# Retention samples as outer products on VectorE, products in parts, the last projection in thirds

## The chip, the cores and the metric

One core of one Trainium2 chip. The metric is the device time of one execution in microseconds (us), as a median over runs.

## The reference

One inference step of a one-layer decoder for a prompt (1024 tokens) and eight samples of one new token each, with the same weights. Retention and forgetting attention run side by side, are merged, normed, and followed by a convolutional feed-forward network and a second norm. The parts that the change touches, cut down:

```python
def retention_chunkwise(q, k, v, s0):      # 4 heads, dk = 128, dv = 256; chunks of 128 tokens, a sample is a chunk of one
    def step(s, qkv):
        qc, kc, vc = qkv
        inner = einsum('bihd,bjhd->bhij', qc, kc) * intra
        o = einsum('bhij,bjhe->bihe', inner, vc) + einsum('bihd,bhde->bihe', qc * q_decay, s)
        s = s * chunk_decay + einsum('bjhd,bjhe->bhde', kc * k_decay, vc)
        return s, o
def merge_branches(...):                   # group norm of ret_o, silu(rg) * rn; sigmoid(ga) * u_a + sigmoid(gb) * u_b
def conv_ffn(h, ...):                      # a = gelu(conv(h @ w_up)) * (h @ w_gate); a @ w_down, d_ff = 2816
def post_norm_ffn(...):                    # layer_norm(ALPHA * h + f): the norm that ends the step
```

The samples' new states (8 x 4 x 128 x 256) are outputs too. The samples' attention reads 32 pages of 128 cached keys and values each, from a page table.

## The kernel before, in words

Activations are held transposed, `x[128, 8, 1032]` (1024 prompt columns and 8 samples), once as a rounded high part and once as the rest. A product (`product`, L106 to L123) is one tile of 128 output columns of a weight matrix: three chunks of 344 columns, each 8 k-tiles x 3 matmuls (high-high, high-low, low-high), 72 matmuls. Products are numbered as jobs. Their weights go through a ring of two: GpSimd loads a tile (`load_weight`, L89) once the tile two jobs back has been split, ScalarE rounds it (`split_hi`, L97), VectorE takes the rest (`split_lo`, L104), and TensorE starts. Chunk n of a product goes to bank n, and the next product waits until that bank has been read.

`retain` loops over four heads. In a head, jobs 0 and 1 are rq and rk (rotated by VectorE), 2 and 3 a gate, 4 and 5 a second gate, 6 and 7 rv, 8 and 9 rg; jobs 10 to 13 are the next head's 0 to 3, so a pass through the loop holds ten products. After job 7 TensorE turns nine blocks of key and value rows (L941, L943), does eight chunks (scores and state update L968 and L969, output L957 and L959), the eight samples, product 8, nine transposes of the normed rows (L1002), and products 9 to 13. The prompt's state is updated by VectorE (L1232), rows are copied by ScalarE (L1060 to L1068), the group norm is VectorE's (L1255 to L1267) and the copy to `rv_t` ScalarE's (L1084). The samples: VectorE makes a masked copy of the eight key rows (L1242) and of the queries (L1244), TensorE multiplies each masked key block with the value rows (L984), VectorE adds that to the decayed state (L1248), and TensorE sums the outputs over eight masked queries (L989).

Between these, in fixed doses (`VALUES_A`, `KEYS_A`, `VALUES_B`, `KEYS_B`: so many groups at each place of the program), VectorE scores cached keys (L1118, L1122) and TensorE multiplies cached values (L889), groups of two pages that SyncE loads into rings of four.

`finish` ends with the feed-forward network in three sections of 8, 7 and 7 of the 22 tiles; each ends with a down projection of eight products that VectorE adds to `acc` (L1720). After the last, nine row blocks are turned by TensorE (L1490, two buffers), measured by VectorE (L1739), normed by ScalarE (L1589), scaled by VectorE (L1731), and get their bias from GpSimd (L1439).

## Time and profile before

| | |
|---|---|
| median of 3 runs | 2246.5 us (2238.74 to 2246.7) |
| the profiled execution, own time | 2241.36 us |
| its span, first to last instruction | 2239.7 us |
| TensorE busy | 2054.5 us (92%) |
| VectorE, ScalarE, GpSimd busy | 1148.9, 614.5, 211.2 us |
| mean granted clock of TensorE | 0.949 of full speed |
| moved by DMA | 266.09 MB, 119 GB/s over the span |

A matmul's busy time overlaps the next one's; what one costs is read from the distance of their starts. The granted clock has two values here, 1.0 (2.4 GHz) and 0.5 (1.2 GHz), and a stretch shows their mean. Its records lie some us behind the matmuls that they slow down.

### The profile page before, as it was taken

To read this page: it belongs to the slowest core of one execution; us is meant where nothing else is said; L and a number is where in the kernel's file an instruction comes from. 1 tells how busy PE (TensorE), PEld (TensorE's weight loads), DVE (VectorE), ACT (ScalarE), POOL (GpSimd) and SP (SyncE) were. 2 spreads that over 40 slices of the span, in tenths; PEclk is the share of its full clock that TensorE was granted. 3 is DMA by queue.
4 is the path that set the end of the run, shared out by engine and by line. 5 is a ranking of instruction groups with operands and counts; after the bars stand their busy time and mean duration, and the time that the engine had idled before them with its cause. 6 is when DMAs were issued, how large, how long until landed. Compare 5 with 4: busy or idle time off the path is not lost. (4 is left out here: it accounts for less than half of the span.)

```text
span 2239.7 us, 39810 instructions
## 1 busy us (share of the span) xinstructions
PE 2054.5 (92%) x14403; PEld 1887.1 (84%) x14403; DVE 1148.9 (51%) x1754; ACT 614.5 (27%) x1127; POOL 211.2 (9%) x241
## 2 busy tenths in 40 slices
PE   7998998798998999899869899699999999999995
PEld 6887888686886787698669889599999999999995
DVE  4645546866847756676432575833332333233326
ACT  4444432123122222222220100444411232023213
POOL 1000000110110020011000010300000000000003
PEclk9999999898999999899879999899999999999997
DMA  4111113693876678489442321011111111111111
GB/s 133 48 38 39 39 38 124 220 320 128 305 264 215 212 257 290 141 285 318 155 158 86 111 86 43 0 57 47 47 47 47 47 47 42 53 42 43 58 46 76
DMA packets 127296, 266.09 MB, mean 119 GB/s; under 512 B 18329, under 2 KB 31734, under 8 KB 127150
## 3 DMA queue, kind: packets, MB, share of 16 engines
q1 hardware_dynamic: 97130, 168.87, 22.1%
q0 software_dynamic: 21856, 78.18, 11.6%
q10 hardware_dynamic: 8192, 17.40, 2.1%
q8 instruction: 82, 1.34, 0.3%
q14 instruction: 36, 0.29, 0.0%
HBM read 236.27 MB, written 28.22 MB: 118 GB/s over the span
## 5 line engine op out<-in xcount | busy, mean ns | idle before, releaser
L121 PE MATMUL bank<-x_hi,w_hi 128*128 128x344 f32 (+1 forms) x2328 | 770.3, 331 | 61.4 <-DVE w_lo L104 16.0
L121 PE MATMUL bank<-x_lo,w_hi 128*128 128x344 f32 (+1 forms) x2328 | 754.5, 324 | 0.0
L121 PE MATMUL bank<-x_hi,w_lo 128*128 128x344 f32 (+1 forms) x2328 | 754.4, 324 | 0.0
L121 PEld LDWEIGHTS bank<-x_hi,w_hi 128*128 128x128 f32 (+1 forms) x2328 | 445.3, 191 | 90.1 <-issue 80.8
L121 PEld LDWEIGHTS bank<-x_lo,w_hi 128*128 128x128 f32 (+1 forms) x2328 | 445.0, 191 | 1.6
L121 PEld LDWEIGHTS bank<-x_hi,w_lo 128*128 128x128 f32 (+1 forms) x2328 | 444.8, 191 | 1.7
L121 PE MATMUL bank<-moving_hi,w_hi 128*128 128x344 f32 x912 | 283.0, 328 | 26.5 <-DVE moving_lo L1595 14.3
L97 ACT ACTIVATE w_hi<-w_raw 128x1024 fp32r<-128x1024 f32 (+2 forms) x145 | 148.6, 1025 | 534.5 <-PE bank L121 491.2
L121 PE MATMUL bank<-moving_lo,w_hi 128*128 128x344 f32 x912 | 292.8, 321 | 0.0
L121 PE MATMUL bank<-moving_hi,w_lo 128*128 128x344 f32 x816 | 263.3, 323 | 0.0
L104 DVE TENSOR_TENSOR w_lo<-w_raw,w_hi 128x1024 fp32r<-128x1024 f32 (+2 forms) x145 | 171.9, 1186 | 138.4 <-ACT w_hi L97 132.8
L121 PEld LDWEIGHTS bank<-moving_hi,w_hi 128*128 128x128 f32 x912 | 170.1, 191 | 36.5 <-issue 16.3
L121 PEld LDWEIGHTS bank<-moving_lo,w_hi 128*128 128x128 f32 x912 | 172.7, 189 | 0.1
L1118 DVE TENSOR_TENSOR cache_keys<-cache_keys,q_wide 128x1024 f32<-128x1024 f32 x128 | 156.5, 1223 | 23.3 <-DMA cache_keys<-in_cache_k_dram 23.3
L121 PEld LDWEIGHTS bank<-moving_hi,w_lo 128*128 128x128 f32 x816 | 155.5, 191 | 0.0
L1122 DVE TENSOR_REDUCE score<-cache_keys 128x16 f32<-128x1024 f32 x128 | 154.8, 1212 | 0.0
L1698 DVE SCALAR_TENSOR_TENSOR stage<-stage,conv_cols_tile 128x1024 f32<-128x1024 f32 x22 | 28.3, 1285 | 186.0 <-ACT stage L1560 186.0
L1720 DVE TENSOR_TENSOR acc<-acc,bank 128x344 f32 (+1 forms) x72 | 36.9, 513 | 168.3 <-PE bank L121 168.3
L89 POOL DMA_DIRECT2D w_raw<-in_w_in_dram x53 | 49.7, 938 | 774.1 <-DVE w_lo L104 585.2
L889 PE MATMUL bank<-cache_vals,score 128*2 128x128 f32 x2048 | 81.5, 278 | 3.0 <-DMA cache_vals<-in_cache_v_dram 2.9
L1708 DVE TENSOR_TENSOR stage<-stage,bank 128x344 f32<-128x344 f32 x66 | 33.8, 512 | 94.8 <-PE bank L121 92.6
L1555 ACT ACTIVATE stage<-bank 128x344 f32<-128x344 f32 x66 | 30.0, 456 | 155.0 <-PE bank L121 155.0
(247 smaller groups left out, 2206.6 us busy)
## 6 DMA issues: line engine op xcount, KB each, us to landing
cache_keys<-in_cache_k_dram SPq DMA_DIRECT2D x256, 256.0 KB, 5.0
cache_vals<-in_cache_v_dram SPq DMA_DIRECT2D x256, 256.0 KB, 5.2
w_raw<-in_w_in_dram POOLq DMA_DIRECT2D x52, 512.0 KB, 7.1
w_raw<-in_w_up_dram POOLq DMA_DIRECT2D x22, 512.0 KB, 4.5
w_raw<-in_w_gate_dram POOLq DMA_DIRECT2D x22, 512.0 KB
gate_t_scratch<-rv_rows ACTq DMA_DIRECT2D x16, 516.0 KB, 4.8
gate<-gate_t_scratch SPq DMA_DIRECT2D x16, 516.0 KB, 3.5
w_raw<-in_w_down_dram POOLq DMA_DIRECT2D x16, 448.0 KB, 4.2
```

Source lines behind the costliest of these rows:

```text
L89: eng.dma_start(g.w_raw[slot][:, 0:kt, 0:m], src).then_inc(g.w_land[slot], 16)
L97: act.activation(g.w_hi[slot][:, 0:kt, 0:m], g.w_raw[slot][:, 0:kt, 0:m], ACT.Copy).then_inc(g.w_rounded, 1)
L104: dve.tensor_tensor(g.w_lo[slot][:, 0:kt, 0:m], g.w_raw[slot][:, 0:kt, 0:m], g.w_hi[slot][:, 0:kt, 0:m].bitcast(F32), ALU.subtract).then_i ...
L121: mm = pe.matmul(g.bank[n][0:m, 0:TC], w[slot][:, k, 0:m], x[:, k, chunk(n)], start=(k == 0 and i == 0), stop=(k == kt - 1 and i == 2))
L889: mm = pe.matmul(bank[7][32 * j:32 * j + 2, 0:P], score[u][:, i * GRP + p, 2 * j:2 * j + 2], vals[slot][:, p, j * P:(j + 1) * P], start=(f ...
L1118: dve.tensor_tensor(keys[slot][:], keys[slot][:], qb[u][:].unsqueeze(1).to_broadcast([P, GRP, FH * HD]), ALU.mult).then_inc(k_mult, 1)
L1122: dve.tensor_reduce(score[u][:, (i - 1) * GRP:i * GRP, :], keys[slot][:].rearrange("p g (h e) -> p g h e", e=HD), AX.X, ALU.add).then_inc( ...
L1555: act.activation(up[:, 2 + k * TC:2 + (k + 1) * TC], bank[k][:, 0:TC], ACT.Copy).then_inc(g.bank_free[k], 1)
L1698: dve.scalar_tensor_tensor(act_in[:, 0:SEQ], up[:, 1:1 + SEQ], fc[:, 17:18], act_in[:, 0:SEQ], ALU.mult, ALU.add).then_inc(conv, 1)
L1708: dve.tensor_tensor(act_in[:, chunk(k)], act_in[:, chunk(k)], bank[k][:, 0:TC], ALU.mult).then_inc(g.bank_free[k], 1)
L1720: dve.tensor_tensor(cols, cols, bank[k][:, 0:TC], ALU.add).then_inc(g.bank_free[k], 1)
```

## The change

1. **Samples.** The samples' value rows go to HBM and come back as two transfers that put four of the rows into every partition (into `inner` and `qd`, which the chunks no longer need then). ScalarE scales the old states, VectorE adds key column x value row (one instruction a sample). The outputs come from matmuls with two columns each in four column groups of the array; the query tile `q_pair` has zeros in the other column.
2. **Parts.** Products 6 to 9 are cut into 24 parts of three matmuls, which stand between the row transposes, the chunks, the samples and the norm's transposes. The second gate's jobs change places with rv's, and the gates are activated and stored chunk by chunk.
3. **Thirds, bias.** The last section's down projection runs over 384, 384 and 264 columns one after the other, each with all eight output tiles (24 jobs with a load and a split each); the rows of a finished third are turned, normed, scaled and get their bias (GpSimd) during the next.

The doses of cached keys and values are moved to fit. The diff, cut (the lines left out rename sizes and drop the masks' constants):

```diff
+def product_part(g, pe, jb, xh, xl, i, kt=KD, m=P):
+    j, slot = jb
+    n, k = i // kt, i % kt
+    if i == 0:
+        pe.wait_ge(g.w_split, RING + j + 1)
+    if k == 0:
+        pe.wait_ge(g.bank_free[n], j + 1)
+    for q, (w, x) in enumerate(((g.w_hi, xh), (g.w_hi, xl), (g.w_lo, xh))):
+        mm = pe.matmul(g.bank[n][0:m, 0:TC], w[slot][:, k, 0:m], x[:, k, chunk(n)],
+                       start=(k == 0 and q == 0), stop=(k == kt - 1 and q == 2))
+    if k == kt - 1:
+        mm.then_inc(g.mm_chunk, 1)
...
-VALUES_A = (1,) * 12 + (1,) * 3 + (1,) + (0,) * 6
-KEYS_A = (1,) * 12 + (1,) * 3 + (1,) + (0,) * 6
-VALUES_B = (0, 1) + (1,) * 3 + (0,) * 3 + (1,) * 12
-VALUES_B_LAST = (2,) * 8 + (0,) * 12
+PARTS = NCH * KD
+VALUES_A = (1, 2, 1, 1, 2, 1) + (0, 1, 1, 0, 1, 1, 0, 1, 1) + (1, 0, 1, 0, 0, 0, 0)
+KEYS_A = (1, 2, 1, 1, 2, 1) + (0, 1, 1, 0, 1, 1, 0, 1, 1) + (1, 0, 1, 0, 0, 0, 0)
+VALUES_B = (1, 1, 1, 1) + (0, 0, 0) + (1,) + (1,) * 7 + (2, 2)
+VALUES_B_LAST = (2,) * 8 + (0,) * 9
...
-        kmask = inner[0:NS]
-        qmask = sb("q_own", [P, NS, NS])
+        spread = [x[:].rearrange("p t d -> p (t d)").rearrange("p (b d) -> p b d", d=DV) for x in (inner, qd)]
+        HALF, GROUPS = NS // 2, 4
+        q_pair = sb("q_own", [P, NS, 2])
...
-        COLS = (C_RQ, C_RK, C_GA, C_GA + P, C_GB, C_GB + P, C_RV, C_RV + P, C_RG, C_RG + P)
+        COLS = (C_RQ, C_RK, C_GA, C_GA + P, C_RV, C_RV + P, C_GB, C_GB + P, C_RG, C_RG + P)
...
-                    for j in (8, 9):
-                        load(h, j)
+                    load(h, 8)
+                    wait_apart(pool, rows_out, (h + 1) * NB, g.mm_chunk)
+                    pool.dma_start(g.v_dram[ds(h, 1)].rearrange("a b d -> (a b) d"), vrows[0:NS, QB, :]).then_inc(v_spread, 16)
+                    load(h, 9)
+                    wait_apart(pool, v_spread, h * 48 + 16, g.mm_chunk)
+                    wait_apart(pool, o_mm, h * NB + QB, g.mm_chunk)
+                    for i in range(2):
+                        rows = g.v_dram[ds(h, 1), i * HALF:(i + 1) * HALF].rearrange("a b d -> a (b d)").to_broadcast([P, HALF * DV])
+                        pool.dma_start(spread[i].rearrange("p b d -> p (b d)"), rows).then_inc(v_spread, 16)
...
+                    parts(6, share(PARTS, NB, 0))
...
+                        if t:
+                            parts(6, share(PARTS, NB, t))
...
+                    parts(7, range(3))
...
+                        if t < QB - 1:
+                            parts(7, range(3 * t + 3, 3 * t + 6))
...
-                    pe.wait_ge(masks, h * 2 + 2)
-                    pe.wait_ge(st_new, (h + 1) * QB)
-                    for b_ in range(NS):
-                        if b_ >= 2:
-                            pe.wait_ge(s_new, h * NS + b_ - 1)
-                        pe.matmul(bank[4 + b_ % 2][:, 0:DV], kmask[:, b_, :], vrows[0:NS, QB, :], start=True, stop=True).then_inc(kv_s, 1)
+                    parts(8, range(4))
+                    for i in range(2):
+                        parts(8, range(4 + 4 * i, 8 + 4 * i))
                     values_b(0)
                     pe.wait_ge(o_out, h * NB + QB)
-                    for b_ in range(NS):
-                        pe.wait_ge(s_new, h * NS + b_ + 1)
-                        mm = pe.matmul(bank[3][0:NS, 0:DV], qmask[:, b_, :], st_s[:, b_, :], start=(b_ == 0), stop=(b_ == NS - 1))
+                    pe.wait_ge(masks, h + 1)
+                    for i in range(2):
+                        pe.wait_ge(s_new, h * NS + (i + 1) * HALF)
+                        for j in range(GROUPS):
+                            b_ = i * HALF + j
+                            mm = pe.matmul(bank[3][32 * j:32 * j + 2, 0:DV], q_pair[:, b_, :], st_s[:, b_, :], start=(i == 0), stop=(i == 1))
                     mm.then_inc(o_mm, 1)
                     values_b(1)
-                    product(g, pe, job(h * NJ + J0, 1, 8), g.xh, g.xl, after=lambda n: values_b(2 + n))
+                    parts(8, range(12, PARTS))
+                    values_b(2)
+                    parts(9, range(8))
+                    values_b(3)
 
                     for t in range(NB):
-                        n = P if t < QB else NS
+                        n = P
                         b = bank[3] if t % 2 == 0 else bank[6]
+                        if t < 8:
+                            parts(9, (8 + t,))
...
+                    parts(9, range(16, PARTS))
+                    values_b(7)
...
+                def gate_chunk(j, i, h, tile, n):
+                    b = i % 2
+                    act.wait_ge(gate_stored[b], h * 96 + (16 * (i // 2) + 1))
+                    chunk_ready(g, act, j, n)
+                    act.activation(sg[b][:], bank[n][:, 0:TC], ACT.Sigmoid).then_inc(g.bank_free[n], 1)
+                    act.wait_ge(g.bank_free[n], j + 2)
+                    act.dma_start(g.gate_dram[ds(tile, 1), :, chunk(n)].rearrange("a p t -> (a p) t"), sg[b][:]).then_inc(gate_stored[b], 16)
...
+                        if t < NS:
+                            act.activation(st_s[:, t, :], st_s[:, t, :], ACT.Copy, scale=hc[:, RDEC]).then_inc(s_scaled, 1)
+                        if t in (1, 4, 6):
+                            gate_chunk(h * NJ + (J0 + 7), 9 + (1, 4, 6).index(t), h, h * 2 + (KD + 1), (1, 4, 6).index(t))
                         if t == QB - 1:
                             cache_exp(h * 2 + 1, 1)
                             nxt(8)
+                            for b_ in range(2):
+                                act.wait_ge(gate_stored[b_], h * 96 + 97)
+                            silu(0)
...
+                    silu(1)
+                    nxt(9)
...
+                    silu(2)
+                    silu(3)
+                    store_gated(0)
+                    silu(4)
+                    silu(5)
+                    store_gated(1)
...
-                    dve.wait_ge(o_mm, h * NB + QB)
-                    dve.tensor_tensor(kmask, krows[0:NS, QB, :].unsqueeze(1).to_broadcast([NS, NS, DK]),
-                                      own[:].unsqueeze(2).to_broadcast([NS, NS, DK]), ALU.mult).then_inc(masks, 1)
-                    dve.tensor_tensor(qmask[:], rqT[:, SEQ:T].unsqueeze(1).to_broadcast([P, NS, NS]), own_col[:], ALU.mult).then_inc(masks, 1)
-                    dve.wait_ge(s_land, h * 16 + 16)
+                    for i in range(2):
+                        pair = slice(i * HALF, (i + 1) * HALF)
+                        ins = dve.tensor_copy(q_pair[:, pair, i], rqT[:, SEQ + i * HALF:SEQ + (i + 1) * HALF])
+                    ins.then_inc(masks, 1)
+                    dve.wait_ge(v_spread, h * 48 + 48)
                     for b_ in range(NS):
-                        dve.wait_ge(kv_s, h * NS + b_ + 1)
-                        dve.scalar_tensor_tensor(st_s[:, b_, :], st_s[:, b_, :], hc[:, RDEC], bank[4 + b_ % 2][:, 0:DV], ALU.mult, ALU.add).then_inc(s_new, 1)
+                        dve.wait_ge(s_scaled, h * NS + b_ + 1)
+                        dve.scalar_tensor_tensor(st_s[:, b_, :], spread[b_ // HALF][:, b_ % HALF, :], rkT[:, SEQ + b_:SEQ + b_ + 1],
+                                                 st_s[:, b_, :], ALU.mult, ALU.add).then_inc(s_new, 1)
...
+    JT, KT = sections[-1][3], sections[-1][1]
+    THIRD = 3
+    EDGE = (0, 3 * P, 6 * P, T)
+    tail = [(i, i // KD, i % KD) for i in range(NCH * KD)]
+    turned_after = {KD * (t // THIRD + 1) + 1 + 2 * (t % THIRD): t for t in range(2 * THIRD)}
...
+                for i, _, m in tail:
+                    load_weight(g, pool, job(JT, JT % 2, i), tile_of(a["w_down"], m, sections[-1][0], KT), KT)
+                    if i - 6 in turned_after:
+                        add_row(turned_after[i - 6])
+                for t in range(QB):
+                    if t not in [turned_after[i - 6] for i, _, _ in tail if i - 6 in turned_after]:
+                        add_row(t)
...
+                def turn_rows(t):
                     n = P if t < QB else NS
+                    pe.wait_ge(g.bank_free[0], JT + 1 + KD * (t // THIRD + 1))
...
+                for i, third, m in tail:
+                    j, slot = job(JT, JT % 2, i)
+                    lo, hi = EDGE[third], EDGE[third + 1]
+                    pe.wait_ge(g.w_split, RING + j + 1)
+                    if i < NCH:
+                        pe.wait_ge(g.bank_free[i], JT + 1)
+                    else:
+                        pe.wait_ge(g.bank_free[0], JT + 1 + i - NCH + 1)
+                    for k in range(KT):
+                        if i == 0:
+                            pe.wait_ge(a_lo, sections[-1][0] + k + 1)
+                        for q, (w, x) in enumerate(((g.w_hi, gh), (g.w_hi, gl), (g.w_lo, gh))):
+                            mm = pe.matmul(bank[i % NCH][:, 0:hi - lo], w[slot][:, k, :], x[:, k, lo:hi],
+                                           start=(k == 0 and q == 0), stop=(k == KT - 1 and q == 2))
+                    mm.then_inc(g.mm_chunk, NCH)
+                    if i in turned_after:
+                        turn_rows(turned_after[i])
+                for t in range(2 * THIRD, NT):
+                    turn_rows(t)
...
+                for i, third, m in tail:
+                    if i < len(tail) - 1:
+                        split_lo(g, dve, job(JT, JT % 2, i + 1), KT)
+                    lo, hi = EDGE[third], EDGE[third + 1]
+                    chunk_ready(g, dve, JT + i, NCH - 1)
+                    dve.tensor_tensor(acc[:, m, lo:hi], acc[:, m, lo:hi], bank[i % NCH][:, 0:hi - lo], ALU.add).then_inc(g.bank_free[0], 1)
+                    for after, step in ((1, measure_rows), (2, invert_rows), (3, scale_rows)):
+                        if i - after in turned_after:
+                            step(turned_after[i - after])
+                for t in range(2 * THIRD, NT):
+                    measure_rows(t)
+                    scale_rows(t - 1)
+                    invert_rows(t)
```

What it moves. On TensorE, the samples of a head (`state_samples` are the states, `inner_t` held the masked keys). Before:

```order
L959 MATMUL banks<-state,q_decayed_t 128x256
L906 MATMUL bank<-ident,dec_out 128x128
L979 REGISTER_ALU
L980 REGISTER_ALU
L984 MATMUL banks<-rv_rows,inner_t 128x256 x8
L989 MATMUL banks<-state_samples,q_own 8x256 x8
L886 ISA
L889 MATMUL bank<-cache_vals,score 2x128 x8
L112 REGISTER_ALU
L121 MATMUL bank<-x_hi,w_hi 128x344
```

The outer products (L984) and the outputs (L989) stood right behind the last chunk, and product 8 (L121) behind them. Now, between two pieces of product 8 (L138):

```order
L138 MATMUL bank<-x_hi,w_lo 128x344
L138 MATMUL bank<-x_hi,w_hi 128x344
L138 MATMUL bank<-x_lo,w_hi 128x344
L138 MATMUL bank<-x_hi,w_lo 128x344
L904 REGISTER_ALU
L906 ISA
L909 MATMUL bank<-cache_vals,score 2x128 x8
L1020 MATMUL banks<-state_samples,q_own 2x256 x8
L909 MATMUL bank<-cache_vals,score 2x128 x8
L138 MATMUL bank<-x_hi,w_hi 128x344
```

The outer products are gone and the outputs (L1020) have 2 rows each; twelve parts of product 8 stand in front of the samples' outputs, and the other twelve behind.

On TensorE, the group norm's transposes of a head. Before, they stood together, without matmuls between. Now (`cache_vals` is a group of cached values):

```order
L909 MATMUL bank<-cache_vals,score 2x128 x8
L138 MATMUL bank<-x_hi,w_hi 128x344
L138 MATMUL bank<-x_lo,w_hi 128x344
L138 MATMUL bank<-x_hi,w_lo 128x344
L1037 MATMUL banks<-ident,rv_rows 128x128 x2
L138 MATMUL bank<-x_hi,w_hi 128x344
L138 MATMUL bank<-x_lo,w_hi 128x344
L138 MATMUL bank<-x_hi,w_lo 128x344
L1037 MATMUL banks<-ident,rv_rows 128x128 x2
L138 MATMUL bank<-x_hi,w_hi 128x344
L138 MATMUL bank<-x_lo,w_hi 128x344
```

A part of product 9 stands in front of each of the first eight.

On GpSimd, the body of the head loop behind the weight load of job 9, before (`w_raw` is the ring's tile):

```order
L89 DMA w_raw<-in_w_in_dram 128x8x128
L73 REGISTER_ALU
L89 ISA
L89 DMA w_raw<-in_w_in_dram 128x8x128
L73 ISA
L838 ISA
L838 ISA cache_max_all<-cache_max 128x8
```

The load of job 10 and the maximum over all partitions (`cache_max_all`) followed directly. The same place now:

```order
L89 DMA w_raw<-in_w_in_dram 128x8x128
L73 REGISTER_ALU
L73 ISA
L886 DMA inner_t<-own_values_scratch 128x1024
L886 ISA
L886 DMA q_decayed_t<-own_values_scratch 128x1024
L73 REGISTER_ALU
L89 ISA
L89 DMA w_raw<-in_w_in_dram 128x8x128
L73 ISA
L851 ISA
L851 ISA cache_max_all<-cache_max 128x8
```

The two spreads (`own_values_scratch` to `inner_t` and `q_decayed_t`) stand in front of both; the store of the value rows, not shown, went in front of load 9.

On GpSimd, the end of the program (`y` with a number is a block of rows), where before all adds of the bias stood behind the last weight load:

```order
L89 DMA w_raw<-in_w_down_dram 128x7x128 x16
L1510 TENSOR_TENSOR y_9124<-y_9124,ln_wide_9134 128x1024
L89 DMA w_raw<-in_w_down_dram 128x7x128 x2
L1510 TENSOR_TENSOR y_9125<-y_9125,ln_wide_9134 128x1024
L89 DMA w_raw<-in_w_down_dram 128x7x128 x2
L1510 TENSOR_TENSOR y_9126<-y_9126,ln_wide_9134 128x1024
L89 DMA w_raw<-in_w_down_dram 128x7x128 x4
L1510 TENSOR_TENSOR y_9127<-y_9127,ln_wide_9134 128x1024
L1510 TENSOR_TENSOR y_9128<-y_9128,ln_wide_9134 128x1024
```

Three adds stand between the weight loads now.

## Rows read from the trace of the kernel before

**Rows 1.** Busy time by stretch: one pass of the head loop.

```profile
core 0: us, PE busy (x) PEld busy (x) DVE busy (x) ACT busy (x) POOL busy (x), PEclk, DMA share, GB/s
624.50:681.70 57.20, 57.05 (x480) 51.64 (x480) 33.83 (x30) 9.69 (x16) 7.98 (x13) 0.95 0.75 254
681.70:688.70 7.00, 5.70 (x75) 3.66 (x75) 4.71 (x4) 5.29 (x18) 0.00 (x0) 1.00 1.01 376
688.70:705.20 16.50, 14.04 (x97) 10.78 (x95) 11.53 (x26) 2.78 (x9) 0.40 (x1) 1.00 0.76 259
705.20:720.50 15.30, 13.10 (x50) 5.75 (x49) 11.03 (x23) 3.32 (x5) 1.08 (x1) 0.67 0.13 35
720.50:734.00 13.50, 13.50 (x121) 12.19 (x120) 8.11 (x24) 1.51 (x3) 0.00 (x0) 1.00 0.52 167
734.00:740.00 6.00, 3.39 (x22) 1.81 (x18) 0.00 (x0) 5.50 (x16) 0.00 (x0) 1.00 0.00 0
740.00:811.10 71.10, 68.47 (x569) 62.36 (x569) 56.82 (x71) 13.41 (x22) 6.78 (x9) 0.95 0.83 277
811.10:815.10 4.00, 0.04 (x1) 0.01 (x1) 0.59 (x3) 3.35 (x5) 0.00 (x0) 1.00 0.83 308
```

**Rows 2.** Busy time by stretch: last head from its samples, down projection, norm.

```profile
1077.90:1119.10 41.20, 35.27 (x351) 24.54 (x354) 15.89 (x43) 10.61 (x23) 0.00 (x0) 0.83 0.57 184
...
2124.60:2201.40 76.80, 76.68 (x486) 76.39 (x486) 20.22 (x32) 7.66 (x7) 4.86 (x5) 1.00 0.14 44
2201.40:2239.70 38.30, 14.94 (x72) 11.33 (x72) 31.00 (x47) 16.85 (x36) 18.74 (x8) 0.58 0.28 111
```

**Rows 3.** The chain that ended last: start, us, what.

```profile
1472.70 22.66 PE bank L121 x144
```

**Rows 4.** Timeline of TensorE after the loop's end, matmul by matmul.

```profile
625.28 0.49 PE L121 MATMUL bank<-x_hi,w_lo 128*128 128x344 f32 x1
...
625.57 0.49 PE L121 MATMUL bank<-x_hi,w_hi 128*128 128x344 f32 x1
```

**Rows 5.** Timeline of TensorE, two groups of cached values, a chunk apart.

```profile
603.26 0.62 PE L889 MATMUL bank<-cache_vals,score 128*2 128x128 f32 x16
...
607.77 0.62 PE L889 MATMUL bank<-cache_vals,score 128*2 128x128 f32 x16
```

**Rows 6.** Timeline, seams: a state's update, a table load, product 9, `finish`.

```profile
713.69 0.48 DVE L1248 SCALAR_TENSOR_TENSOR state_samples<-state_samples,head_const,banks 128x256 f32<-128x256 f32 x1 [0.37 <-PE banks L984]
...
740.71 1.28 ACT L1093 ACT_TABLE_LOAD   x1
...
742.61 0.63 PE L121 MATMUL bank<-x_hi,w_hi 128*128 128x344 f32 x1 [2.71 <-ACT rot_cos L1093]
...
1141.63 11.58 SPq L1378 DMA_DIRECT2D gated_raw<-gated_t_scratch  x8
```

**Rows 7.** DMA issues: KB each, median us from issue to landing.

```profile
q_wide<-q_new_scratch SPq DMA_DIRECT2D x8, 256.0 KB, 5.4
```

**Rows 8.** Weight loads of L89 within the last down projection (448 KB).

```profile
DMA to landing us min/median/max: 4.2/4.3/4.4
```

**Rows 9.** Timeline, one weight tile's rounding, split, and the next load's issue.

```profile
2132.04 1.06 ACT L97 ACTIVATE w_hi<-w_raw 128x1024 fp32r<-128x1024 f32 x1 [7.71 <-PE bank L121]
...
2133.14 1.23 DVE L104 TENSOR_TENSOR w_lo<-w_raw,w_hi 128x1024 fp32r<-128x1024 f32 x1 [0.47 <-ACT w_hi L97]
...
2135.09 0.96 POOL L89 DMA_DIRECT2D w_raw<-in_w_down_dram  x1 [7.64 <-DVE w_lo L104]
```

**Rows 10.** Timeline of the final norm: scaling (VectorE), bias (GpSimd).

```profile
2206.93 1.22 DVE L1731 TENSOR_TENSOR y<-y,ln_wide 128x1024 f32<-128x1024 f32 x1 [0.22 <-ACT y L1589]
...
2208.25 2.34 POOL L1439 TENSOR_TENSOR y<-y,ln_wide 128x1024 f32<-128x1024 f32 x1 [42.47 <-DVE y L1731]
...
2209.89 1.78 DVE L1731 TENSOR_TENSOR y<-y,ln_wide 128x1024 f32<-128x1024 f32 x1
...
2213.41 1.77 DVE L1731 TENSOR_TENSOR y<-y,ln_wide 128x1024 f32<-128x1024 f32 x1
```

192 lines of the change are left out of this document (101 added, 91 removed).

## The prediction

> **What bounds the kernel now.** I read the page first: TensorE is busy for nearly all of the span, so time can only come from stretches where it idles, runs at its lower clock or does work that something else could have covered. Then I cut one iteration of the head loop of `retain` into its stages with the busy time by stretch [rows 1], the last head and the end of the kernel likewise [rows 2], and went into the timeline only at the seams.
>
> The reader is to see three things in [rows 1]. The first 57.2 us and the stretch from 740.0 to 811.1 are dense products. Between them lie 52.3 us in which TensorE is short of work in small doses: row transposes, the eight retention chunks, then 15.3 us for eight samples at a mean granted clock of 0.67, and 6.0 us of group norm in which it is busy for 3.4. Last, 4.0 us of nothing at the loop's end, after which the next stretch shows a clock of 0.95: 2 x 0.05 x 57.2, or 6 us, at the lower level of 1.2 GHz.
>
> Prices. At 2.4 GHz 144 matmuls take 22.66 us [rows 3], 0.157 each: a product (72) is 11.3 us, a chunk of it (24) 3.77, a part (3) 0.47. At 1.2 GHz one starts every 0.29 us [rows 4]. A group of cached values behind a chunk costs 4.51 (from 603.26 to 607.77, [rows 5]) less 3.77, or 0.75, of which 0.55 is the group.
>
> **The change, part by part.** All sums are against the profiled execution (span 2239.7, own time 2241.4 us); the median of the runs shown is 2246.5, 5.1 more, and I take the gain off that.
>
> *Rows and chunks, products 6 and 7 in parts .* Before, from the first product to the last output 57.2 + 7.0 + 16.5 = 80.7 us. After, TensorE's work is the same: four products 45.2, 3 lost at the low clock, 16 value groups 12.0, nine row transposes at 0.38, eight chunks at 1.52, 0.8 for the tail of the sums; what goes are the waits on ScalarE and VectorE (5.7 and 14.0 us busy in 7.0 and 16.5), what comes are some 17 seams between products and small matmuls, at 0.1 each (half the 0.19 that a value group pays beyond its own 0.55). Sum 78.5: **-2** a head. It would be no more if the parts were free, because before, too, the products themselves ran at full rate.
>
> *Samples.* Gone are the two masks, the eight outer products on TensorE and the eight 8-column matmuls, at the low clock. Now VectorE needs the value rows in all partitions. GpSimd issues two 512 KB spreads, and only after the last chunk's output, since they land in `inner` and `qd`. From that moment (705.2 before): issue 0.9 + 0.9, landing, eight updates at 0.4 (one took 0.48 with overlap, [rows 6]) = 3.2. The landing is not in the trace; the nearest are 4.3 us for 448 KB of weights on the same queue [rows 8] and 5.4 for a 256 KB row spread in the same way while the cache streams [rows 7]. Lower end 3.5 (as for 448 KB without its issue), upper end 8 (twice the bytes of the spread row, its fixed part once); I take 4.5, as the cache stream is idle there (DMA share 0.13). States ready at 0.1 + 1.8 + 4.5 + 3.2 = 9.6. TensorE's cover: 12 parts of product 8 and one group, 5.65 + 0.75 = 6.4. So it waits 3.2. Then the outputs, 16 passes in four column groups, 1 us with seams; a group, the other 12 parts, a group, 8 parts of product 9, a group: 12.2. It arrives at the first normalised row at 22.8; VectorE needs for `nxt(8)`, the first keys and nine statistics about 12 us after the states (19.1 busy in 705.2 to 734.0 less 7 for masks and states), 21.6: no wait. The nine rows, a part with each, at 0.9: 30.5. Before, to the same point (740.0), 15.3 + 13.5 + 6.0 = 34.8: **-4.3**. Moving `all_max` behind the spreads costs nothing here: it is done by 3.2, before the states could start. Queued behind VectorE's wait for the spreads are `nxt(8)` and the statistics; I have counted them.
>
> *Product 9 under the group norm.* Before 71.1 us from 740.0: five products, twelve groups, 2.7 of waiting for the gate activation (742.61, [rows 6]) and the low clock after it. After: four products and a third, 49.0, twelve groups 9.0, 1.0 for the tail; chunk 2 of product 9 still waits for bank 2, which `silu(2)` frees behind the last row and a table load of 1.28 [rows 6], 2.3 us; 0.5 where product 11 catches up with the rotations. Sum 61.8: **-9.3**. This is the term that leans on VectorE: it was busy for 56.8 of the 71.1 us [rows 1], so in 61.8 it is at 92%.
>
> Together -15.6 for each of the first three heads. The last has no product 10 to 13 but all 16 value groups early: -2; 41.2 -> 37.8; and from 1119.1 [rows 2] to the first load of `finish` at 1141.6 [rows 6], 22.5 -> 13.3 (chunk 2 with its wait 6.1, two groups, turn, store): **-14.6**. `retain`: 3 x 15.6 + 14.6 = -61.4.
>
> *Low clock at new seams.* A new wait of 3.2 us followed by 2-column matmuls, and one of 2.3 after the group norm, are like the places before which the trace drops to 1.2 GHz (2.71 us idle at 742.61, then [rows 1] 0.95). One drop costs 6 us at 0.29 in place of 0.157, 2.7 us. Two places, four heads; I count every second one: **+11**.
>
> *Thirds.* The last down projection becomes 24 jobs: 21 matmuls of 384, 384 and 264 columns, 3.68 and 2.6 us by the column from 0.157. Every job loads, rounds and splits its weights again. A slot's cycle is landing 4.3 [rows 8] + 0.1 + 3.05 from the rounding to the next issue (2132.04 to 2135.09, [rows 9]) - 0.28 for 7/8 of the columns = 7.2 for two jobs, 3.6 a job. So thirds one and two run at TensorE's 3.68, the last at the load's 3.6 where TensorE needs 2.6. Of the first job only the last matmuls are left at 2124.6: 15.2 x 3.68 + 8 x 3.6 = 84.7; three iterations in which VectorE measures one row and scales another (1.5 + 1.8) before it can split hold the next job for 1.2 each, GpSimd's adds (2.34, [rows 10]) hold a load for 1.3. Sum 90 against 76.8 [rows 2]: +13. Behind it only rows 6 to 8 are left: six fewer at 3.52 (2209.89 to 2213.41, [rows 10]), less 1.8 for row 5's scaling in front: 38.3 -> 19.1. Net **-6**.
>
> A rule bears on this. In [rows 10] the first scaling takes 1.22, the next 1.78: it begins at 2209.89, GpSimd's add ends at 2210.59, and 1.08 later VectorE is done. So VectorE was held until GpSimd was through. The Trainium skill (SBUF - State Buffer, "SBUF: two separate sides") says the same: the pair of ports is an exclusive lock, and a VectorE operation with two SBUF inputs blocks while GpSimd reads. By it each of the adds now inside the jobs can hold a weight split for up to 2.34 us: four of them, +9, and the tail would be +3 in place of -6. I keep -6, since GpSimd's adds mostly start while VectorE waits for a product; the other is a rival.
>
> Sum: -61.4 + 11 - 6 = -56: 2246.5 - 56 = **2190**.
>
> **Rivals.** A, *the moved product does not come free*: VectorE, at 92%, and the key loads (a DMA share of 0.83 in [rows 1], 0.96 when squeezed into 61.8) set the pace from 740 on; product 9 then gives 3 us in place of 9.3 in each of three heads, +19: 2209. For it: the two rates are so near. Against: no key wait of size stands in this stretch before. B, *all of it*: no new seam drops the clock and the spreads land at 3.5: 2190 - 11 - 4 = 2175. For it: TensorE idled over 2 us within the chunks at a clock of 1.00. C, *the port lock eats the tail*: 2190 + 9 = 2199. D, *no change to speak of*: what TensorE is spared comes back as waits for the cache stream, 2240 to 2252; against it, the share of 0.76 and 0.13 in the chunks and the samples. E, *slower*: interleaved with small matmuls, the products of 6 to 9 run at 1.2 GHz. Price: 288 matmuls x 0.13 = 37 us a head, 149 in all, so 2190 - 11 + 149 = 2328 if all do; it decides from the point at which 45% of them (67 of 149) are slow. Against: in the chunk stretch, with 2.5 us idle, the clock was 1.00 [rows 1]. The Trainium skill (TensorE: Matmul & The Clock Gate, "What's actually happening") has the low clock as the default that activity lifts; it would speak for E only if interleaved work counted as idle, which no row shows. A second page, TensorEngine Tiling ("Key Properties"), says that changing the tiling mode drains the array; the 0.19 around a value group is what the trace shows of that, and it is in the seams.
>
> **The numbers.** Forecast 0.41, A 0.19, B 0.16, C 0.10, D 0.06, E 0.08. Predicted 2190. The upper end adds to the forecast the other half of the clock drops (+11), spreads at 8 us (+14) and part of A: 2220; the lower end is B with a little over: 2170. What lies outside is D, E and the far end of A. Within 0.5% (11 us, what a measurement of this kernel can tell) only D: 0.06; slower 0.08; faster 0.86.
>
> **What would show it.** Right: in a head, rows and chunks at a clock of 1.00 with TensorE over 95% busy; `state_samples` matmuls in 1 us after 2 to 4 us of idling released by VectorE's updates; v_spread landing 4 to 5 us after issue; the head's period 175 us (190.6 before) and 64 instead of 71 us behind the group norm; in the tail, jobs every 3.7 us, TensorE waiting for `w_lo` in the last third, 19 us behind the last product. Wrong: idle time before product 11 or 12 released by the rotations or by key loads (A); granted clock 0.5 inside products 6 to 9 (E); jobs of 5 us in the tail with `w_lo` behind GpSimd's adds (C); period unchanged with DMA share at 1 (D). The forecast itself fails most easily in the wait for the spreads, whose landing no row shows, and in how often the clock falls.

## The result, and the profile after

The changed kernel takes 2220.32 us (median of 4 runs, 2217.56 to 2223.97) against 2244.85 for the kernel before in the same comparison: ratio 0.9906, 95% interval 0.9884 to 0.9927, so it is faster by 21 us (16 to 26) by the ratio; the two medians differ by 24.5. The prediction said 2190 (2170 to 2220). The direction was right; the gain was less than half of the 56 us that were forecast.

The page of the changed kernel: busy times of TensorE to GpSimd.

```profile
span 2215.5 us, 39880 instructions
...
PE 2009.2 (91%) x14335; PEld 1873.5 (85%) x14335; DVE 1159.2 (52%) x1771; ACT 645.5 (29%) x1175; POOL 240.9 (11%) x269
```

TensorE works 45 us less (2054.5 before), but the span fell by 24.2 only: 21 us more in which it idles. The pass of head 1 again, cut at the places of [rows 1] (the columns are the same; stages: two whole products, rows, chunks, then up to the samples' outputs, up to the norm's first transpose, the transposes, the dense part, the loop's turn):

```profile
624.34:654.84 30.50, 30.50 (x272) 27.80 (x273) 20.32 (x18) 3.68 (x8) 9.15 (x11) 0.91 0.70 237
654.84:682.37 27.53, 22.78 (x207) 19.11 (x204) 15.93 (x14) 9.96 (x24) 1.51 (x2) 0.88 0.83 286
682.37:706.15 23.78, 23.78 (x175) 21.04 (x174) 14.30 (x28) 6.04 (x16) 0.00 (x0) 1.00 0.80 271
706.15:721.93 15.78, 8.80 (x70) 6.45 (x72) 4.92 (x14) 5.64 (x9) 2.40 (x4) 0.79 0.37 112
721.93:735.57 13.64, 13.64 (x116) 12.16 (x109) 11.64 (x32) 3.40 (x5) 1.08 (x1) 0.87 0.61 204
735.57:741.10 5.53, 5.28 (x39) 4.61 (x36) 2.41 (x5) 5.12 (x15) 0.88 (x1) 1.00 0.15 21
741.10:806.50 65.40, 58.81 (x523) 53.41 (x523) 55.38 (x70) 12.03 (x19) 6.58 (x8) 1.00 0.83 279
806.50:810.60 4.10, 0.28 (x4) 0.01 (x1) 0.32 (x2) 3.11 (x4) 0.00 (x0) 1.00 1.05 355
```

The chunks (third row) are full, as the parts were meant to make them. Three rows have holes: 4.75 us in the row transposes, 7.0 in front of the samples' outputs, and 6.6 in the dense part (2.6 in the 71.1 us before). The timeline names them, TensorE's waits in head 1 (in brackets: us idle, and what ended it; two more that `rot_sin` ended, 0.48 at 762.65 and 0.95 at 779.99, are not shown):

```profile
661.88 1.03 PE L909 MATMUL bank<-cache_vals,score 128*2 128x128 f32 x16 [3.75 <-DMA cache_vals<-in_cache_v_dram]
...
717.98 1.03 PE L909 MATMUL bank<-cache_vals,score 128*2 128x128 f32 x16 [5.90 <-ACT score L1057]
719.63 0.61 PE L1020 MATMUL banks<-state_samples,q_own 128*2 128x256 f32 x4 [0.62 <-DVE state_samples L1311]
...
744.02 0.42 PE L138 MATMUL bank<-x_hi,w_hi 128*128 128x344 f32 x1 [2.47 <-ACT rot_cos L1087]
...
774.46 0.42 PE L121 MATMUL bank<-x_hi,w_hi 128*128 128x344 f32 x1 [1.91 <-DVE rot_sin L1246]
```

The wait that I had expected in front of the outputs, for the states, is 0.62 us there, and 0.46 in front of their second half. The big one is one instruction earlier: a group of cached values waits 5.90 for the softmax's exponential (L1057). Followed back, first GpSimd, then VectorE:

```profile
706.96 0.56 POOL L886 DMA_DIRECT2D inner_t<-own_values_scratch  x1 [24.80 <-PE banks L988]
707.56 0.55 POOL L886 DMA_DIRECT2D q_decayed_t<-own_values_scratch  x1
708.31 0.91 POOL L89 DMA_DIRECT2D w_raw<-in_w_in_dram  x1 [0.20 <-issue]
716.53 0.39 POOL L851 PARTITION_ALL_REDUCE cache_max_all<-cache_max  x1 [7.32 <-issue]
...
716.96 0.43 DVE L1203 TENSOR_TENSOR score<-score,cache_max_all 128x264 f32<-128x264 f32 x1 [11.19 <-POOL cache_max_all L851]
717.31 0.33 DVE L1219 COPY fox_sample_t<-bank 64x4 f32 x2
717.67 0.24 DVE L1306 COPY q_own<-rq_t 128x4 f32<-128x4 f32 x2
717.82 1.67 DVE L1311 SCALAR_TENSOR_TENSOR state_samples<-inner_t,rk_t,state_samples 128x256 f32<-128x256 f32 x4
```

The maximum over all partitions has its scores since 699.6 and takes 0.39 us by its record, but starts 7.3 us after the weight load in front of it, with nothing shown that it waits for. VectorE stands 11.19 us at it, and the states, whose value rows had landed at about 713, follow behind. The same line on its own shows what fills the 7.3 us (start times of the first and last record):

```profile
L851 POOLq MODIFY_POOL_CONFIG  x2: 37/37/37, 709.5 to 709.5; - x2
L851 POOL PARTITION_ALL_REDUCE cache_max_all<-cache_max x1: 394/394/394, 716.5 to 716.5; - x1
```

GpSimd is set up for this instruction at 709.5 and begins 7.0 us later. In the kernel before the set-up stands at 672.1, long before the scores are ready, and so it is hidden:

```profile
L838 POOLq MODIFY_POOL_CONFIG  x2: 37/37/37, 672.1 to 672.1; - x2
L838 POOL PARTITION_ALL_REDUCE cache_max_all<-cache_max x1: 397/397/397, 699.4 to 699.4; - x1
```

The Trainium skill (GPSIMD Engine Reference, "2.1 Instruction dispatch") says so: the first call of a freshly loaded GpSimd function pays about 6 us between `MODIFY_POOL_CONFIG` and its start, with no instruction visible in the profile. The trace agrees in kind, with 7.0 us; the length differs, and it is paid more than once. The program runs two GpSimd functions in a head, eight multiplications (L876) and the maximum, and the set-up stands at every change between them: the multiplications of the four heads start 8.9, 11.1, 10.4 and 9.7 us after theirs. The next maximum of the same head, with no other function in between, has no set-up record and starts 0.2 us after its scores:

```profile
L851 POOL PARTITION_ALL_REDUCE cache_max_all<-cache_max x1: 1172/1172/1172, 613.6 to 613.6; - x1
```

A rival for the 7.0 us is work that GpSimd might still have with the three transfers issued just in front. Against it: where its function does not change, an operation starts 0.02 us after a weight load's issue (an add at 2176.80 in experiment 4, behind a load of 2175.80 to 2176.78). How the 7.0 us divide was not tested.

The end of the kernel, from the last down projection's first matmul (2100.0) on, took 115.5 us; before it was 118.4 (2121.3 to 2239.7). The jobs took 97.3 in place of 80.1, what follows them 18.2 in place of 38.3. The rows of it that matter, VectorE's splits beside GpSimd's adds:

```profile
2155.10 3.16 POOL L1510 TENSOR_TENSOR y<-y,ln_wide 128x1024 f32<-128x1024 f32 x1 [4.08 <-DVE y L1843]
...
2154.93 1.08 DVE L104 TENSOR_TENSOR w_lo<-w_raw,w_hi 128x896 fp32r<-128x896 f32 x1
2156.63 2.58 DVE L104 TENSOR_TENSOR w_lo<-w_raw,w_hi 128x896 fp32r<-128x896 f32 x1
...
2166.68 0.59 PE L1583 MATMUL bank<-moving_hi,w_hi 128*128 128x264 f32 x1 [2.90 <-DVE w_lo L104]
```

### The profile page after: what moved, and what is told of

Same layout as the page of the kernel before. It is cut to its first block and busy times, and to the rows that moved or that the text cites. A ratio compares the mean times of both kernels' runs of the same rounds, so it can differ in the third digit from the quotient of the medians.

```text
span 2215.5 us, 39880 instructions
## 1 busy us (share of the span) xinstructions
PE 2009.2 (91%) x14335; PEld 1873.5 (85%) x14335; DVE 1159.2 (52%) x1771; ACT 645.5 (29%) x1175; POOL 240.9 (11%) x269
## 3 DMA queue, kind: packets, MB, share of 16 engines
q0 software_dynamic: 25184, 89.75, 13.5%
## 5 line engine op out<-in xcount | busy, mean ns | idle before, releaser
L121 PE MATMUL bank<-x_hi,w_hi 128*128 128x344 f32 (+1 forms) x1944 | 639.6, 329 | 58.6 <-DVE w_lo L104 18.3
L121 PE MATMUL bank<-x_lo,w_hi 128*128 128x344 f32 (+1 forms) x1944 | 629.3, 324 | 0.0
L121 PE MATMUL bank<-x_hi,w_lo 128*128 128x344 f32 (+1 forms) x1944 | 629.3, 324 | 0.0
L121 PEld LDWEIGHTS bank<-x_hi,w_hi 128*128 128x128 f32 (+1 forms) x1944 | 370.6, 191 | 77.6 <-issue 65.7
L121 PEld LDWEIGHTS bank<-x_lo,w_hi 128*128 128x128 f32 (+1 forms) x1944 | 370.4, 191 | 1.6
L121 PEld LDWEIGHTS bank<-x_hi,w_lo 128*128 128x128 f32 (+1 forms) x1944 | 370.3, 190 | 1.7
L97 ACT ACTIVATE w_hi<-w_raw 128x1024 fp32r<-128x1024 f32 (+3 forms) x161 | 163.0, 1012 | 574.8 <-PE bank L121 386.9
L121 PE MATMUL bank<-moving_hi,w_hi 128*128 128x344 f32 x744 | 229.9, 331 | 25.4 <-DVE moving_lo L1708 13.7
L104 DVE TENSOR_TENSOR w_lo<-w_raw,w_hi 128x1024 fp32r<-128x1024 f32 (+3 forms) x161 | 192.3, 1194 | 110.4 <-ACT w_hi L97 98.4
L121 PE MATMUL bank<-moving_lo,w_hi 128*128 128x344 f32 x744 | 239.4, 322 | 0.0
L121 PE MATMUL bank<-moving_hi,w_lo 128*128 128x344 f32 x648 | 210.0, 324 | 0.0
L121 PEld LDWEIGHTS bank<-moving_hi,w_hi 128*128 128x128 f32 x744 | 139.0, 192 | 35.0 <-issue 16.1
L138 PE MATMUL bank<-x_hi,w_hi 128*128 128x344 f32 x384 | 142.5, 371 | 8.0 <-ACT rot_cos L1087 8.0
L121 PEld LDWEIGHTS bank<-moving_lo,w_hi 128*128 128x128 f32 x744 | 141.4, 190 | 0.1
L138 PE MATMUL bank<-x_lo,w_hi 128*128 128x344 f32 x384 | 127.7, 333 | 0.0
L138 PE MATMUL bank<-x_hi,w_lo 128*128 128x344 f32 x384 | 127.7, 332 | 0.0
L121 PEld LDWEIGHTS bank<-moving_hi,w_lo 128*128 128x128 f32 x648 | 124.3, 192 | 0.0
L89 POOL DMA_DIRECT2D w_raw<-in_w_in_dram x53 | 49.9, 943 | 634.4 <-DVE w_lo L104 431.0
```

What stands on the lines that cost most here:

```text
L89: eng.dma_start(g.w_raw[slot][:, 0:kt, 0:m], src).then_inc(g.w_land[slot], 16)
L97: act.activation(g.w_hi[slot][:, 0:kt, 0:m], g.w_raw[slot][:, 0:kt, 0:m], ACT.Copy).then_inc(g.w_rounded, 1)
L104: dve.tensor_tensor(g.w_lo[slot][:, 0:kt, 0:m], g.w_raw[slot][:, 0:kt, 0:m], g.w_hi[slot][:, 0:kt, 0:m].bitcast(F32), ALU.subtract).then_i ...
L121: mm = pe.matmul(g.bank[n][0:m, 0:TC], w[slot][:, k, 0:m], x[:, k, chunk(n)], start=(k == 0 and i == 0), stop=(k == kt - 1 and i == 2))
L138: mm = pe.matmul(g.bank[n][0:m, 0:TC], w[slot][:, k, 0:m], x[:, k, chunk(n)], start=(k == 0 and q == 0), stop=(k == kt - 1 and q == 2))
```

## The experiments

All ratios are to the kernel before, run beside each on the same chip; one step of 0.001 is 2.2 us, and the intervals are about 0.002 wide to each side, 0.004 in experiments 9, 10 and 11. The changed kernel, experiments 1 to 4, 5 to 8, 9 to 11 and 12 come from a comparison each; the difference of two ratios is uncertain by some 5 or 6 us, and by some 10 with one of 9 to 11.

**1. The maximum in front of the spreads.** One line of GpSimd's program is moved.

```diff
                     load(h, 9)
+                    all_max(h * 2 + 1)
                     wait_apart(pool, v_spread, h * 48 + 16, g.mm_chunk)
...
                         load(h, NJ)
-                    all_max(h * 2 + 1)
```

> Only GpSimd's order is changed: the maximum over all partitions of the second sample's scores is issued in front of the two spreads instead of behind them. Theory 1 (queue order): in the profile of the changed kernel the value group in front of the samples' outputs waits 5.8 to 6.5 us a head for the softmax's exponential, which waits for that maximum, and the maximum is done 9.6 us after the last chunk because the spreads' issue stands in front of it. Moved, it is done at about the last chunk's end; then TensorE waits for the states only, which follow the spreads' landing: 3.7 us in place of 7.5 a head, so 15 us less, 2205 (ratio to the kernel before 0.982). Theory 2 (the spreads are the wait anyway): VectorE would stand at the spreads as long as it stands at the maximum now, 2217 to 2221 and no change.

Measured: 2195.0, ratio 0.9804 (0.9787 to 0.9820), against 0.9906: 23 us of gain from one line, more than the 15 expected. The waits for the exponential are gone, and TensorE waits for the states, 1.96 and 0.46 us in the first head, 1.98 and 0.88 in the second. All waits in front of the samples' outputs come to 2.4 to 2.9 us a head, where the theory had 3.7. Stage by stage, 20.6 of the 22.0 us that `retain` gained lie between the last chunk's output and the last norm transpose (7.4, 4.3, 5.7 and 3.2 in the four heads). VectorE, freed of its 11 us at the maximum, also no longer comes late with the rotations behind the norm (0.48, 1.91 and 0.95 us of waiting for them in head 1 of the changed kernel, none above 0.4 here). But that is worth little: from the last norm transpose to the next pass head 1 takes 68.5 us in place of 69.3, since the granted clock there is 0.94 in place of 1.00:

```profile
729.20:797.24 68.04, 61.19 (x522) 55.93 (x522) 55.82 (x72) 14.54 (x22) 6.58 (x8) 0.94 0.86 289
```

The theory of queue order holds, and the late rotations of head 1 came from VectorE's being held earlier.

**2. Even doses.**

```diff
-VALUES_A = (1, 2, 1, 1, 2, 1) + (0, 1, 1, 0, 1, 1, 0, 1, 1) + (1, 0, 1, 0, 0, 0, 0)
-KEYS_A = (1, 2, 1, 1, 2, 1) + (0, 1, 1, 0, 1, 1, 0, 1, 1) + (1, 0, 1, 0, 0, 0, 0)
+VALUES_A = (1,) * 6 + (0, 1, 1, 0, 1, 1, 0, 1, 1) + (1, 1, 1, 1, 0, 0, 0)
+KEYS_A = (1,) * 6 + (0, 1, 1, 0, 1, 1, 0, 1, 1) + (1, 1, 1, 1, 0, 0, 0)
```

> Only the doses of cached keys and values in the first stretch of a head are changed: one group a chunk in products 4 and 5 (6 in place of 8), and the two left over go into the retention chunks. Theory 1 (SyncE's rate): SyncE issues four pairs of groups in 2.2 us each and then pauses 6 to 7 us at its loop's turn, so it feeds one group each 3.8 us at best; eight groups in the 30 us of two products are right at that, and TensorE waits 4.0 to 7.2 us a head for cached values. Evened, most of it goes, and the clock drops behind these waits too: 12 to 20 us less, 2200 to 2208. Theory 2 (the stream's total): the same waits come back in the row transposes or the chunks, 2217 to 2221.

Measured: ratio 0.9900 (0.9883 to 0.9918), no change. My theory fell: the waits for cached values moved from the first row transposes to later ones (0.48, 0.70 and 2.31 us in head 1, in place of 3.75 and 1.00). The stream as a whole was behind, not a dose.

**3. Early spreads.** The value rows land in `rv_t`, which is idle between its last transpose and the norm.

```diff
-        spread = [x[:].rearrange("p t d -> p (t d)").rearrange("p (b d) -> p b d", d=DV) for x in (inner, qd)]
         HALF, GROUPS = NS // 2, 4
+        spread = [rvT[:].rearrange("p e t -> p (e t)")[:, i * HALF * DV:(i + 1) * HALF * DV].rearrange("p (b d) -> p b d", d=DV) for i in range(2)]
...
                     wait_apart(pool, v_spread, h * 48 + 16, g.mm_chunk)
-                    wait_apart(pool, o_mm, h * NB + QB, g.mm_chunk)
```

> The two spreads land in rv_t, which is free between the last row transpose and the group norm, in place of inner and qd; so they no longer wait for the last chunk's output and are issued some 15 us earlier, and the maximum behind them is early too. Theory 1 (all of the wait in front of the samples' outputs hangs on GpSimd's position behind the last chunk): states ready 3.4 us after the last chunk, value group ready as well, TensorE does not wait there, 7.5 us less a head, 30 in all: 2190 (ratio 0.976). Theory 2 (collision): a megabyte of spreads now falls into the chunks, where the DMA share is 0.8, and 2 to 3 us a head come back as waits for cached values: 2198 to 2202. If the maximum alone mattered, this run and e1_max_first would come out alike.

Measured: 2176.57, ratio 0.9722 (0.9706 to 0.9739), 41 us below the changed kernel, 18 below experiment 1, and lower than either theory said. From the last chunk's output to the last norm transpose the pass now takes 24.6 us (35.0 in the changed kernel, 34.8 before) and TensorE does not stop in it. Windows of head 1, up to the last chunk's output, to the norm's end, to the next pass:

```profile
611.70:692.80 81.10, 77.13 (x650) 68.00 (x650) 51.14 (x60) 19.72 (x47) 12.04 (x17) 0.92 0.82 287
692.80:717.40 24.60, 24.42 (x218) 21.92 (x216) 18.70 (x47) 14.01 (x29) 1.96 (x2) 1.00 0.42 126
717.40:786.50 69.10, 61.80 (x523) 55.78 (x523) 55.64 (x72) 15.20 (x23) 6.57 (x8) 0.93 0.86 290
```

So the wait for the spreads, 3.2 us a head in my sum, was a real second cost behind the maximum, and the collision did not show. The spreads do take longer among the cache's loads (a median of 7.0 us to land, 10.3 at most, in place of 4.8 and 5.6), which costs nothing, since they have some 19 us (673.7 to 692.8 in head 1).

**4. Bias adds behind the last weight load.**

```diff
                 for i, _, m in tail:
                     load_weight(g, pool, job(JT, JT % 2, i), tile_of(a["w_down"], m, sections[-1][0], KT), KT)
-                    if i - 6 in turned_after:
-                        add_row(turned_after[i - 6])
                 for t in range(QB):
-                    if t not in [turned_after[i - 6] for i, _, _ in tail if i - 6 in turned_after]:
-                        add_row(t)
+                    add_row(t)
```

> Only the tail is changed: GpSimd adds the bias of all rows behind the last weight load. Theory 1 (a GpSimd queue that is just full): the two loads that were issued late (TensorE idle 2.9 and 2.7 us) come in time and the splits beside the adds take 1.1 in place of 1.6 to 2.6 us, 6 to 8 us less in the jobs, but nine adds of 2.34 now follow each other from the last load on and end about where they end now: 2214 to 2220, a gain of 0 to 5. Theory 2 (the port lock is the tail's main cost, the rival C of the prediction): 9 us less, 2211.

Measured: ratio 0.9891 (0.9873 to 0.9910), 3 us below the changed kernel and within the intervals: no change that can be told. From the last section's first down matmul to the end the trace has 116.9 us, 1.4 more than the changed kernel's. The loads came in time, but the adds, now in a row, held VectorE. GpSimd and VectorE in this run:

```profile
2176.80 6.98 POOL L1510 TENSOR_TENSOR y<-y,ln_wide 128x1024 f32<-128x1024 f32 x3
...
2177.57 7.31 DVE L1840 TENSOR_TENSOR y<-y,ln_wide 128x1024 f32<-128x1024 f32 x1
2184.80 1.08 DVE L104 TENSOR_TENSOR w_lo<-w_raw,w_hi 128x896 fp32r<-128x896 f32 x1
```

A scaling that takes 1.22 us alone [rows 10] lasted 7.31: it began 0.8 us after the first of three adds and ended 1.1 us after the third. The split behind it came late, and TensorE waited 6.80 us.

**5. Product 9 behind the norm.** From here on, on top of the early spreads.

```diff
-                    parts(9, range(8))
...
-                        if t < 8:
-                            parts(9, (8 + t,))
...
-                    parts(9, range(16, PARTS))
+                    parts(9, range(PARTS))
```

> On top of the early spreads (e3_early_spread: ratio 0.9722, some 2177). The first 16 parts of product 9 are moved from in front of and under the group norm to behind it, where the kernel before had the whole product. Theory 1 (my step: under the norm the parts are free, because VectorE and ScalarE set its length, and VectorE keeps up behind it): 16 x 0.49 = 7.8 us a head come back, 31 in all, 2208 (ratio 0.986). Theory 2 (the prediction's rival A: behind the norm VectorE and the key loads set the pace, so that taking work from that stretch gives little): 0 to 10 us, 2177 to 2187.

Measured: ratio 0.9774 (0.9754 to 0.9794), 12 us above experiment 3 (6 to 18), or 2.9 a head. Far from theory 1 and just above theory 2, whose 10 us lie within the uncertainty: having the parts in front of and under the norm saves 2.9 us and not 7.8. With the product behind the norm, TensorE idles 3.3 us in front of and within the transposes, but the 2.47 us for the gate's activation, which the other order exposes between the parts and the third chunk, are gone. What else takes part of the 7.8 was not separated.

**6. Products 6 and 7 whole.**

```diff
-                    parts(6, share(PARTS, NB, 0))
+                    parts(6, range(PARTS))
...
-                        if t:
-                            parts(6, share(PARTS, NB, t))
...
-                    parts(7, range(3))
+                    parts(7, range(PARTS))
...
-                        if t < QB - 1:
-                            parts(7, range(3 * t + 3, 3 * t + 6))
```

> On top of the early spreads (some 2177). Products 6 and 7 are whole again: 6 in front of the row transposes, 7 between them and the chunks; the doses of the cache keep their places. Theory 1 (my step: the parts only fill the waits of rows and chunks, less what their seams cost): 2 us a head come back, 8 in all, 2185. Theory 2 (the parts hide more than counted, since the chunks' chain over ScalarE and VectorE is then waited for in full): 5 or more a head, over 2195. Theory 3 (the seams eat it): no change.

Measured: ratio 0.9828 (0.9801 to 0.9855), 24 us above experiment 3, 5.9 a head: theory 2. The old waits are back (0.69 and 1.69 us for `inner_t` in the chunks, 1.91 for `rv_rows` in the transposes), and those for cached values are larger, 3.90 and 1.54 us, presumably because without parts the rows and chunks ask for values in a shorter time.

**7. The old tail.** `finish` is that of the kernel before, word for word.

```diff
-                for i, third, m in tail:
...
+                    with pe.Fori(0, KD // 2) as it:
+                        for u in range(2):
+                            product(g, pe, job(it * 2 + jd, jd % 2, u), gh, gl, n, ready=lambda k: pe.wait_ge(a_lo, f0 + k + 1))
```

> On top of the early spreads (some 2177). The feed-forward network's end is that of the kernel before: three chunks a product, eight jobs, all nine rows behind them. The two traces put the thirds at 118.4 to 115.5 us from the last section's first down matmul to the end, so 3 us come back: 2180. Had the thirds cost what rival C said (the port lock), this run would be 3 us faster: 2174.

Measured: ratio 0.9737 (0.9718 to 0.9756), 3 us above experiment 3. The intervals overlap, and the ratio alone shows nothing. The traces do: from the last section's first down matmul to the end, the kernel before and this run both take 118.4 us, the changed kernel 115.5, experiments 1, 2, 3, 5, 8, 9, 11 and 12 take 115.5 to 115.9 and experiment 6 113.9. The thirds gain some 3 us.

**8. Page numbers group by group.** A cause for the late cached values was still open. SyncE's timeline in the changed kernel, around the wait of 3.75 us at 661.88 (the loads of that group are issued in the pairs that follow the gap):

```profile
645.77 1.94 SPq L807 DMA_DIRECT2D cache_keys<-in_cache_k_dram  x2
647.97 0.86 SPq L807 DMA_DIRECT2D cache_vals<-in_cache_v_dram  x2
655.16 0.87 SPq L807 DMA_DIRECT2D cache_keys<-in_cache_k_dram  x2
656.35 0.85 SPq L807 DMA_DIRECT2D cache_vals<-in_cache_v_dram  x2
...
663.24 0.85 SPq L807 DMA_DIRECT2D cache_vals<-in_cache_v_dram  x2
670.42 0.87 SPq L807 DMA_DIRECT2D cache_keys<-in_cache_k_dram  x2
```

Four pairs at 2.2 to 2.4 us, then 6.3 us of nothing (648.83 to 655.16, 664.09 to 670.42): the turn of its loop, where it reads 16 page numbers into registers.

```diff
-                        key_ids, value_ids = page_ids(n + 1, q), page_ids(n, q)
                         for slot in range(SLOTS):
-                            load_group(keys, k_land, k_used, ck, n + 1, q, slot, key_ids)
-                            load_group(vals, v_land, v_used, cv, n, q, slot, value_ids)
+                            load_group(keys, k_land, k_used, ck, n + 1, q, slot, page_ids(n + 1, q, slot))
+                            load_group(vals, v_land, v_used, cv, n, q, slot, page_ids(n, q, slot))
```

> On top of the early spreads (some 2177). SyncE reads the page numbers of a group right in front of the group's loads, two at a time, instead of all 16 of a loop turn at once. Theory 1 (the waits for cached values come from SyncE's pause of 6 to 7 us a turn, not from the DMA engines or the doses): the pauses are spread, the waits of 3 to 6 us a head fall below 2 and with them the clock drops behind: 10 to 18 us less, 2160 to 2167. Theory 2 (SyncE's total of issues and reads is what limits, or the DMA engines are, at a share of 0.8): no change, 2174 to 2180.

Measured: 2248.45, ratio 1.0044 (1.0030 to 1.0057): 72 us above experiment 3, slower than the kernel before. The edit was meant to spread the pauses and made their sum larger. A pair now takes 4.6 to 5.2 us, all the time:

```profile
674.49 0.86 SPq L807 DMA_DIRECT2D cache_keys<-in_cache_k_dram  x2
676.73 0.85 SPq L807 DMA_DIRECT2D cache_vals<-in_cache_v_dram  x2
679.64 0.86 SPq L807 DMA_DIRECT2D cache_keys<-in_cache_k_dram  x2
```

Between two issues lie 1.4 us for two numbers (675.35 to 676.73), so eight reads a turn cost 11 us where two cost 6.3. My theory 1 had the place right and the price of a read wrong; this run shows that a slower SyncE costs time. Whether a faster one gains is what the next asks.

**9. One read for keys and values.**

```diff
-                        key_ids, value_ids = page_ids(n + 1, q), page_ids(n, q)
+                        key_ids = value_ids = page_ids(n + 1, q)
```

> On top of the early spreads (e3_early_spread: ratio 0.9722, some 2176). SyncE reads one list of eight page numbers a loop turn and uses it for the keys and for the values, so the cached values multiplied are those of the wrong pages: the outputs of the cached attention are left wrong, the work is the same but for eight register reads a turn. Theory 1 (SyncE's reads are what makes cached values late; two at a time they cost 71 us): the pause of 6.3 us a turn halves, the waits of 3 to 6 us a head go under 2, 8 to 15 us less: 2161 to 2168. Theory 2 (the DMA engines' share is the bound): 2174 to 2180.

Measured: 2152.36, ratio 0.9611 (0.9572 to 0.9651), 25 us below experiment 3; the gap at a turn is 3.5 us. More than expected, and the waits for cached values between a pass's start and the chunks' end are 1.9 us in the first head and 1.0 in the second (6.4 and 4.0 in experiment 3).

**10. Early spreads and adds behind the loads together.** The diffs of 3 and 4.

> The early spreads and the bias adds behind the last weight load together. If the 3 us of e4_adds_last (ratio 0.9891 against 0.9906) are real, they add: 2173, ratio 0.971. If they were noise: 2176, 0.972.

Measured: ratio 0.9719 (0.9674 to 0.9763): no gain, though this interval is too wide to tell 3 us. The trace is clearer: the tail takes 117.4 us, 1.5 more than in experiment 3, so moving the adds gains nothing.

**11. Product 8 whole, behind the samples' outputs.**

```diff
-                    parts(8, range(4))
-                    for i in range(2):
-                        parts(8, range(4 + 4 * i, 8 + 4 * i))
...
-                    parts(8, range(12, PARTS))
+                    parts(8, range(PARTS))
```

> On top of the early spreads (some 2176). Product 8 is whole again, behind the samples' outputs. Theory 1 (its twelve parts in front are the only cover of the states' 3.4 us on VectorE): TensorE waits 3 to 4 us in front of the samples' outputs in each head, and with the clock behind it 3 to 6 us a head come back: 2188 to 2200. Theory 2 (what TensorE loses there it regains at the group norm, whose statistics are VectorE's and end at the same time): 0 to 1 us a head, 2176 to 2180.

Measured: ratio 0.9814 (0.9777 to 0.9851), 21 us above experiment 3, 5.1 a head (3 to 7), the size that theory 1 gave. But what TensorE stands at is not the states but the value group in front of them, 3.38 us for the exponential in each of three heads and 3.17 in the last.

**12. One list, one read, no bounds checks.** All of this is the whole computation again.

```diff
+        pairs = sb("page_pairs", [1, NS * TURNS, 2, IDS], I32)
...
-                        key_ids, value_ids = page_ids(n + 1, q), page_ids(n, q)
+                        both = nc.values_load_multi_w_load_instructions(
+                            pairs[0:1, ds(n * TURNS + q, 1)].rearrange("p a e i -> p (a e i)"), [mybir.EngineType.SP], min_val=0, max_val=POOL - 1, skip_runtime_bounds_check_because="page numbers are drawn below the pool's size")
+                        key_ids, value_ids = both[0:IDS], both[IDS:2 * IDS]
```

> On top of the early spreads (e3_early_spread: ratio 0.9722). The page numbers for the keys and the values of a loop turn lie side by side in a second list, so that SyncE reads all 16 with one load, and the two bounds checks a number (32 instructions a turn) are left out; nothing of the outputs is left out. Theory 1 (SyncE's pause sets how late cached values are; halving its reads took 25 us): the pause falls from 6.3 to 3 us or less, value waits under 1 us a time, 20 to 35 us less: 0.957 to 0.963, some 2148. Theory 2 (e9_one_read gained by something else, as keys and values from the same pages being cheaper for the DMA engines): no change, 0.972.

Measured: 2147.25, ratio 0.9583 (0.9567 to 0.9599), 31 us below experiment 3, as theory 1 said, and the fastest version of the study (0.0417 of 2242.28, or 94 us, below the kernel before). SyncE at a turn:

```profile
639.72 0.85 SPq L812 DMA_DIRECT2D cache_vals<-in_cache_v_dram  x2
642.38 0.86 SPq L812 DMA_DIRECT2D cache_keys<-in_cache_k_dram  x2
643.57 0.85 SPq L812 DMA_DIRECT2D cache_vals<-in_cache_v_dram  x2
```

The gap is 1.8 us (640.57 to 642.38), and in the four heads one wait for cached values over 0.4 us is left (1.67, in the last). TensorE's mean granted clock over the program is 0.968, 0.954 in the changed kernel. In head 1, from the pass's start to the last chunk's output (81.8 us in the changed kernel, 80.7 before), TensorE does not stop:

```profile
604.44:677.95 73.51, 73.51 (x649) 65.45 (x650) 50.54 (x60) 19.65 (x46) 14.07 (x17) 0.98 0.87 305
```

The loads moved at 305 GB/s there, where the changed kernel had 263, so the DMA engines were not what made the values late. The Trainium skill (Runtime: NRT & Kernel Launch, "Instruction fetch mechanics") puts a register load, which it describes from HBM, at about 200 ns a register even in bulk; here, from SBUF, 16 in 1.8 us are at most 0.11 each. How much of the 4.5 us saved belongs to the second load and how much to the 32 checks was not separated.

## Why the prediction was wrong, point by point

**What bounds the kernel** was read rightly: time came only from TensorE's thin stretches. Of the forecast 56 us the profiled spans show 24.2: `retain`, from the first job in the head loop (434.7 before, 435.9 after) to the first product of `finish` (1147.7 and 1125.3), 23.6 in place of 50.4.

| term, one of the first three heads (measured in head 1) | forecast | measured | what it was |
|---|---|---|---|
| rows and chunks | -2 | +1.1 (80.7 to 81.8) | waits for cached values, 4.75 us |
| samples, to the last norm transpose | -4.3 | +0.2 (34.8 to 35.0) | wait behind the maximum, 5.9 us |
| behind the norm | -9.3 | -5.6 (75.1 to 69.5) | rotations 3.3, values 0.7 us late |
| low clock at new seams | +2.7 | in the rows above | mean over `retain` 0.93, then 0.94 |
| sum | -12.9 | -4.3 | |

1. **"Moving `all_max` behind the spreads costs nothing here: it is done by 3.2"** is the step that failed first. I priced the maximum by its record and did not look at what GpSimd does between the set-up and the record, which the order of before had hidden. It is done 10.8 us after the last chunk, holds the value group 5.8 to 6.5 us in each head and VectorE 11. Experiment 1 gives 23 us back with that one line: most of the 30 us by which the prediction missed. Of "queued behind VectorE's wait" the sum had counted `nxt(8)` and the statistics; the rotations behind the norm came late too, in head 1, but the 3.3 us of waiting for them turned into time at the low clock when they were gone (experiment 1).

2. **Rows and chunks** failed by a wait that the sum had no term for. I took the doses of the cache as TensorE work of 0.75 us each and never asked at what rate SyncE can deliver. The number was in reach: four pairs in 8.9 us and a pause of 6.3 make 3.8 us a group, and the pause stands in the trace of the kernel before as well (651.57 to 657.89):

```profile
649.86 1.71 SPq L794 DMA_DIRECT2D cache_vals<-in_cache_v_dram  x2
657.89 0.86 SPq L794 DMA_DIRECT2D cache_keys<-in_cache_k_dram  x2
```

Before, a group was asked for every 4.5 to 5 us; the changed kernel asks for eight in 30.5 us and goes on through rows and chunks. Experiments 8, 9 and 12 show it: the time follows SyncE's pause in both directions (+72, -25, -31 us). The waits also cost clock: 0.91 and 0.88 in the first two rows of the table of stages, about 12 us at the lower level, against some 6 before. On the other hand the parts of products 6 and 7 are worth 5.9 us a head and not 2 (experiment 6): against my sentence that free parts would bring no more, the small matmuls' waits on ScalarE and VectorE are what they hide, 4.3 us in head 1, beside 1.5 us more of late values there. Both errors lie in one term, with opposite signs: without late values the stretch takes 73.5 us (experiment 12), 7.2 less than before.

3. **Samples.** The landing of the spreads was sized well (4.8 and 5.6 us measured; I took 4.5), the outputs in 2.3 with the second half's wait of 0.5 us (I took 1), the eight updates in 3.3 (3.2). The wait of 3.2 us did not show because a longer one stood in front of it; with the maximum moved it is there, as 1.9 to 2.9 us. Experiment 3 shows what it and its cause, buffers that are free only behind the last chunk, are worth: 18 us. Two slips in the sum nearly cancel: the groups and parts behind the outputs make 11.7 and not 12.2, nine rows at 0.9 make 8.1 and not 7.7. The twelve parts of product 8 as cover are worth 5.1 a head (experiment 11).

4. **Product 9 under the norm** was mis-sized: 5.6 us measured behind the norm in head 1; the parts themselves are worth 2.9 a head (experiment 5). The wait of 2.3 us for the gate is there as forecast, 2.47, in three heads. The 2.9 are the 3 that rival A priced, but its cause, a pace set by VectorE or the key loads, is not what the traces show: in head 0 of the changed kernel TensorE waits for neither behind the norm, and in experiment 3 it idles 7.1 of 68.5 us there, 4.5 for the loop's turn and 2.5 for the gate. VectorE is close, though: in experiment 12, with shorter passes, waits of 0.9 and 1.3 us for the rotations are back in two heads. What else takes from the 9.3 is in part the low clock (0.93 there in experiment 3), and was not separated.

5. **The last head** came out as forecast: 14.1 us (forecast 14.6), from its first product (1000.2 before, 991.9 after, by counting the products behind the norm) to that of `finish`. The first three gave 1.4, 4.3 and 3.8, in place of 15.6 each less the clock term. As the last head, too, waits 5.8 us behind the maximum and 5.0 for cached values, its agreement is in part luck.

6. **The low clock** cost nothing more than before. The +11 was a term for seams that drop the clock. Stage by stage in head 1 the low clock moved: rows and chunks 0.95 to 1.00 before and 0.88 to 1.00 after, samples 0.67 and then 0.79, product 8 1.00 and then 0.87, the dense part 0.95 and then 1.00.

7. **Thirds**: 2.9 us by the two traces (some 3 in the others), forecast 6. Mis-sized were the jobs, +17.2 us where the sum had +13; the rows behind them came out, -20.1 against -19.2. The port lock of rival C exists (the split of 2.58 us above, three more of 1.61 to 2.04, in place of 1.09, and adds of 3.2 in place of 2.34), as the Trainium skill (SBUF - State Buffer, "SBUF: two separate sides") has it, but these four stretches hold VectorE for 3.6 us in all (7.92 less 4 x 1.09), and not nine on the path; experiments 4 and 10 find nothing to win by moving the adds, since in a row they held VectorE longer.

8. **A reading of [rows 1].** "Between them lie 52.3 us" leaves out the norm's 6.0 and takes in the 13.5 of product 8, in which TensorE is full. No term hangs on it.

Of the rivals, E (products at 1.2 GHz) is out: the chunks run at 1.00. A's time, 2209, was the nearest to 2220, by another mechanism. D named waits for the cache stream, and they are what point 2 found, but it put them down to the DMA engines and not to SyncE.

## What to carry to other kernels

Before an instruction is moved on a queue, read what stands in front of its record and not only its duration: here 7 us behind a set-up record of 0.04 were free only as long as the engine came early. When work is packed closer, compare its demand with the rate at which the issuing engine can feed it, over that engine's full cycle with the pause at its loop's turn; an engine that computes nothing was worth more here (31 us) than the whole change (21). And a buffer that is reused at the last possible moment ties a load to the critical path; a search for one that is idle earlier took two lines and gave 18 us.

## What the runs showed of the hardware

GpSimd's maximum over partitions starts 7.0 to 7.6 us after its set-up record when nothing hides that, in all four heads, and the multiplications that alternate with it 8.9 to 11.1 us after theirs; a maximum that follows another has no such record and starts 0.2 us after its scores. Reading page numbers into SyncE's registers costs 6.3 us for two reads of eight with their bounds checks, 3.5 for one read of eight, 1.4 for a read of two, and 1.8 for one read of 16 without checks. Beside each other a GpSimd add and VectorE's split of a weight both stretch, from 2.34 to 3.16 us and from 1.09 to 2.58; and in experiment 4 a VectorE scaling with two inputs that met three adds in a row ended 1.1 us after the third (7.31 us in place of 1.22).
